# The norm of kk in a hybrid RWKV-7 and sliding-window attention block: products of 32 columns and a spread by 64-row products

## The chip, the cores and the metric

The kernel runs on one core of a Trainium2 chip. The metric is the device time of one execution in microseconds; lower is better. A core has a matrix engine (PE, whose weight loads are listed as PEld), a vector engine (DVE), a scalar engine (ACT), GpSimd (POOL) and a queue that issues transfers (SP). The engines run their own instruction lists and wait for each other on semaphores.

## The reference, cut to what matters

One decoder block over 1024 tokens and 2048 channels. Its projection feeds 16 RWKV-7 heads and 16 attention heads, all of 64 channels. Of the RWKV part the change touches this:

```python
kk = (k * k_k).reshape(B, T, H, N)                      # N = 64 channels of a head
kk = kk / jnp.maximum(jnp.linalg.norm(kk, axis=-1, keepdims=True), 1e-12)
...
xs = (r, decay, k, v, kk, kk * a)                       # each step of the recurrence
S = S * w_t + sa[..., None] * b_t + v_t[..., None] * k_t   # sa = -S kk_t, b_t = kk_t * a_t
```

The kernel leaves the factor kk * a without its norm and divides the other kk by the squared norm, which is the same product.

## The kernel before, in words

**Layout.** Channels lie on partitions and tokens on columns. The tokens are taken in two halves of 512 (`HALF`, four blocks `b` of 128). A pair of heads is one tile of 128 channels; there are 8 pairs, so 16 intervals `j` (0 to 15), of which the second half of the tokens has 8 to 15.

**The projection and its quarters.** All of the projection and output products go through `quarter` (L1113 is the helper `turn`, a transpose through PE; L1128 is the product of `quarter`). A tile of 128 output channels takes 16 chunks of 128 inputs, in four quarters of four chunks. Each chunk is three products of 128 x 512 (weights and x are split in a high and a low part). A quarter is so 12 products on L1128. The whole kernel is a loop over quarters `gq`, on every engine. An interval has 24 quarters; the number of the quarter within it is `at` in the code, and is called **step** here. Ahead of the 12 products of a step, PE does what `recurrence(j - 1, at)` and then `channels(j, at)` hand it: while interval j has its channels prepared, the recurrence and the attention of interval j - 1 are worked off in the same steps. For j = 0 there is no recurrence beside it, and after j = 15 the last recurrence runs with no channels.

**Pacing.** In step gq ACT makes the high part of the weights of quarter gq + 4 (`high`, L527), for which it waits until PE has finished quarter gq - 1 (its buffers are 5 deep), and DVE then makes the low part (`low`, L717), as its first instruction of the step. So DVE can't begin a step before PE has ended the one before.

**The norm of kk before.** ACT squares k * k_k at step 5 into `s1` (L590).
- Step 10, PE, L1167: for each of the four blocks, a product with the block of `s1` (128 x 128) as weights and the constant `head_of` (128 x 2) as what streams, into two columns of PSUM bank 2 each. A float32 product is two instructions, so these are 8. Result: tokens on partitions, 8 columns (4 blocks, 2 heads).
- Step 11, DVE, at its end: maximum with 1e-24 (L829), reciprocal (L830), copy with broadcast to 128 x 512 in `grow` (L831), then `inv_ready`.
- Step 12, PE, L1113 on the tile `work`: waits for `inv_ready`, four transposes of 128 x 128 from `grow` into bank 3.
- Step 13, DVE, L836: kk = k * k_k * bank 3, then `kk_read`. PE waits for `kk_read` at step 14 (L1280).

**What stands around it.** On PE: step 9 `turn_p(i, 0)`, eight transposes of the first half's attention probabilities (L1113 on `score`), which wait for `p_norm` that DVE gives at the end of `softmax_norm(i, 0)` (L915 to L918, signalled at L920) in step 8. Step 11: `values(i, 0)` (L1261), `turn_kk` (L1222) and level 0 of the inverse (L1271). Step 13: `turn_p(i, 1)`, which waits for the `p_norm` of `softmax_norm(i, 1)`, DVE's first work after `low` in step 12. On DVE: step 9 the output of an earlier interval (L1033, L1035) and scores; step 10 `softmax_top(i, 1)` (L903 to L909), then the eviction of the V tile (L735); step 11 `low`, `attended`, `shift` of v, and the norm.

**Tiles of PE.** Products with 64 columns or 64 rows of weights use a part of the array, and their neighbours another part: L1261 and L1349 have 128 rows x 64 columns (`128*64` in the rows), L1197 64 rows x 128 columns, L1222, L1271, L1280, L1338 and L1368 64 x 64.

**Constants.** `cst` is one tile of 1282 float32 columns, loaded at the start between the second and the third chunk of x. The first product that reads it is L1137 of the first quarter (sum of squares of x), which waits for its landing.

Of the kernel before, what the change touches and what calls it, by code (L numbers as in the profile page):

```python
# [10 lines left out]
ALU = mybir.AluOpType  # L11
# [3 lines left out]
P = 128  # L15
# [3 lines left out]
HD = 64  # L19
PAIRS = 8  # L20
# [46 lines left out]
CONSTS = {}  # L67
_at = 0
for _name, _w in (("ident", 128), ("same_head", 128), ("mean", 128), ("amask", 256), ("m16", 64),
                  ("m32", 64), ("dist", 256), ("dist0", 256), ("head_of", 2)):  # L70
    CONSTS[_name] = (_at, _at + _w)
    _at += _w
CONST_COLS = _at
# [2 lines left out]
def constants():  # L76
    r = np.arange(128)[:, None]
    c = np.arange(128)[None, :]
    t = {}
    t["ident"] = (r == c)  # L80
    t["same_head"] = (r // HD == c // HD)
    t["mean"] = np.full((128, 128), 1.0 / D)
    s, u = r % C, np.arange(C)[None, :]
    t["amask"] = np.concatenate([s <= u, s < u, s < u, s <= u], axis=1)
    for m in (16, 32):
        t[f"m{m}"] = (s // (2 * m) == u // (2 * m)) & (s % (2 * m) >= m) & (u % (2 * m) < m)
    key = np.arange(2 * BT)[None, :]
    d = BT + r - key
    t["dist"] = np.where((d >= 0) & (d < BT), d, 1e33)
    t["dist0"] = np.where((d >= 0) & (d < BT) & (key >= BT), d, 1e33)  # L90
    t["head_of"] = (r // HD == np.arange(2)[None, :])
    return np.concatenate([t[n].astype(np.float32) for n in CONSTS], axis=1)


# [13 lines left out]
def tile_of(i, t):  # L108
    return base(i) // 4 + tile_order(i).index(t)
# [41 lines left out]
def program(nc, io, scr):  # L151
    with ExitStack() as ctx:
        def sb(name, shape, dt=F32):
            return ctx.enter_context(nc.sbuf_tensor(name, shape, dt))
# [13 lines left out]
        own_stage = [sb(f"stage{i}", [P, HALF]) for i in range(3)]  # L168
        work = sb("work", [P, 8, HALF])
        k, a, s1, sw, grow, r, g, sig = (work[:, i] for i in range(8))  # L170
        raw = sb("raw", [P, HALF + 1])
        decay = sb("decay", [P, NCH, C + 1])
        lora = sb("lora", [P, HALF])
# [1 line left out]
        keep = sb("keep", [P, HALF], U8)  # L175
        carry = sb("carry", [P, 4 * PAIRS + 1])
        lora_up = [sb(f"lora_up{i}", [P, P]) for i in range(2)]
        inv2 = sb("inv2", [P, BH])
        pc = sb("pc", [P, 2, NCH])
        eps = sb("eps", [P, 2])  # L180
        sinks = sb("sinks", [P, HEADS])
# [137 lines left out]
        with nc.Block() as block:  # L319
# [387 lines left out]
            def _(dve):  # L707
                count = [0]

                def then(ins):  # L710
                    ins.then_inc(steps, 1)
                    count[0] += 1
                    dve.wait_ge(steps, count[0])
# [80 lines left out]
                def channels(j, at):  # L794
# [20 lines left out]
                    if at == 8:  # L815
# [2 lines left out]
                        then(nc.vector.tensor_tensor(kb[:, :, 0:4:3], a.rearrange(chunks, b=NB, c=2),  # L818
                                                     grow.rearrange(chunks, b=NB, c=2), ALU.mult))
                    if at == 10:  # L820
                        evicted(tile_of(j, V_T), h, 4 * n + 1)
                    if at == 11:
                        shift(v[:], p(n, "mu_v"))
                    if at == 12:
                        dve.wait_ge(s_full, 2 * j)
                        read_tile(tile_of(j, Q_T), q[:], HD ** -0.5)
                    if at == 11:
                        dve.wait_ge(norm_done, 2 * j + 1)
                        then(nc.vector.tensor_scalar(inv2[:], psum[:, 2, 0:BH], 1e-24, None, ALU.max))  # L829
                        then(nc.vector.reciprocal(inv2[:], inv2[:]))  # L830
                        then(nc.vector.tensor_copy(grow.rearrange("p (m d) -> p m d", d=HD),  # L831
                                                   inv2[:].unsqueeze(2).broadcast_to([P, BH, HD])))
                        dve.sem_inc(inv_ready, 1)
                    if at == 13:
                        dve.wait_ge(norm_done, 2 * j + 2)
                        then(nc.vector.scalar_tensor_tensor(k, k, p(n, "k_k"), psum[:, 3], ALU.mult, ALU.mult))  # L836
                        dve.sem_inc(kk_read, 1)
                        for c in range(2):
                            ins = nc.vector.tensor_tensor(
                                qr[:, :, 2 - c], k.rearrange(chunks, b=NB, c=2)[:, :, c],  # L840
                                decay[:, :, 0:C].rearrange("p (b c) t -> p b c t", c=2)[:, :, c], ALU.mult)
                        then(ins)
# [268 lines left out]
            def _(pe):  # L1111
# [28 lines left out]
                def channels(j, at):  # L1140
                    if at == 1:
                        h = j // PAIRS
                        pe.wait_ge(up_landed[j % 2], 16 * (j // 2 + 1))
                        pe.wait_ge(lora_ready, 2 * h + 2)
                        pe.wait_ge(rooted, h + 1)
                        pe.wait_ge(inv_ready, j)
                        pe.wait_ge(bonus_read, j)
                        if j == PAIRS:
                            pe.wait_ge(yt_read, PAIRS - 1)
                        for x in range(2):  # L1150
                            rows = slice(x * LORA, (x + 1) * LORA)
                            nc.tensor.matmul(psum[:, 2 + x], lora_up[j % 2][rows, :], lora[rows, :],
                                             start=True, stop=True).then_inc(lora_done, 1)
                    if at == 4 and j % PAIRS == 0:
                        h = j // PAIRS
                        pe.wait_ge(va_raw, h + 1)
                        pe.wait_ge(sigma_a, j + 1)
                        for b in range(NB):
                            mm = turn(psum[:, 3, b * P:(b + 1) * P], raw[:, 1 + b * P:1 + (b + 1) * P])
                        mm.then_inc(va_full, 1)  # L1160
                    if at == 10:
                        pe.wait_ge(squares, j + 1)
                        pe.wait_ge(sigma_w, j + 1)
                        if j >= 2:
                            pe.wait_ge(yt_read, j - 1)
                        for b in range(NB):
                            mm = nc.tensor.matmul(psum[:, 2, 2 * b:2 * b + 2], s1[:, b * P:(b + 1) * P],  # L1167
                                                  const("head_of"), start=True, stop=True)
                        mm.then_inc(norm_done, 1)
                    if at == 12:  # L1170
                        pe.wait_ge(inv_ready, j + 1)
                        pe.wait_ge(sigma_a, j + 1)
                        if j % PAIRS == 0:
                            pe.wait_ge(va_read, j // PAIRS + 1)
                        for b in range(NB):
                            mm = turn(psum[:, 3, b * P:(b + 1) * P], grow[:, b * P:(b + 1) * P])
                        mm.then_inc(norm_done, 1)
                    if at == 24:
                        pe.wait_ge(rkr_ready, j + 1)
                        pe.wait_ge(kk_read, j + 1)  # L1180
                        nc.tensor.matmul(psum[:, 3], const("same_head"), s1, start=True, stop=True  # L1181
                                         ).then_inc(bonus_done, 1)
# [296 lines left out]
```

## Time and profile before

| | us |
|---|---|
| median of 3 runs | 1952.3 |
| lowest, highest | 1951.01, 1953.26 |
| the profiled execution, its own time | 1952.34 |
| its span in the profile | 1950.6 |
| granted clock of PE, mean | 0.996 of full speed |

The span is that from the first to the last instruction; 1.7 us of the execution's time lie around it. In a row of the timeline the first number is the start in us from the span's start, the second the time from the first start to the last end of the instructions that the row merges, `x8` their count, and `[0.39 <-DVEq L920]` the idle time of that engine before them and what ended it. DVEq is DVE's sequencer: a semaphore raised at that line. PE's instructions overlap, since each is given its whole way through the array: what one costs is read from start to start, not from its duration.

### The profile page before, as it was taken

Reading aid. Unit: us, or ns where it says so; the run is one execution under the profiler, and the core shown is the slowest. Engines: PE = TensorE matmul, PEld = TensorE weight load, DVE = VectorE, ACT = ScalarE, POOL = GpSimd, SP = SyncE. Lnnn points to the kernel's source line nnn. Section 1 sums busy time; section 2 is a strip of 40 time slices with the busy share of each in tenths; the row PEclk is TensorE's granted clock in tenths of the full one; section 3 lists DMA queues with packets and bytes.
Section 4 is the critical chain, followed back from the end, with each engine's and each line's share of the span. In section 5 each row is a group of like instructions: output and inputs, shape, how many; then the busy total and the mean of one; then the engine's idle time right before and its main releaser. Section 6 shows DMA issues by size and latency. Waiting matters only on the chain.

```text
span 1950.6 us, 39494 instructions
## 1 busy us (share of the span) xinstructions
PE 1909.1 (98%) x16000; PEld 1542.0 (79%) x16000; DVE 1240.3 (64%) x2358; ACT 786.7 (40%) x1545; POOL 268.6 (14%) x585
## 2 busy tenths in 40 slices
PE   8999999999999999999999999999999999999996
PEld 5778878788788877788787877888787778888885
DVE  4667576767667677665767676676767764346433
ACT  6434434343434344444343434343434443243221
POOL 0002021120202020020211202020202021111110
PEclk9999999999999999999999999999999999999998
DMA  6533232323333234332323232232323543455533
GB/s 185 168 105 85 80 95 74 101 74 96 81 89 92 81 97 151 104 86 80 96 74 101 74 96 80 90 92 82 93 75 97 163 109 97 130 186 178 165 124 124
DMA packets 208453, 207.25 MB, mean 106 GB/s; under 512 B 114960, under 2 KB 117008, under 8 KB 208272
## 3 DMA queue, kind: packets, MB, share of 16 engines
q1 hardware_dynamic: 208272, 204.73, 35.2%
q8 instruction: 126, 2.06, 0.4%
q14 instruction: 55, 0.45, 0.1%
HBM read 181.08 MB, written 23.59 MB: 105 GB/s over the span
## 4 chain that ended last, share of the span: by engine, by line
PE 90%; DVE 6%; ACT 2%; issue 1%; DMA 1%; DVEq 0%; SPq 0%; ACTq 0%
PE psum L1128 70%; PE psum L1113 3%; PE psum L1280 2%; PE psum L1197 2%; PE psum L1236 2%; PE psum L1261 1%; PE psum L1271 1%; DVE w_lo L717 1%; DVE score L918 1%; PE psum L1385 1%; ACT w_hi L527 1%; PE psum L1349 1%; PE psum L1181 1%; PE psum L1356 1%; PE psum L1222 1%
## 5 line engine op out<-in xcount | busy, mean ns | idle before, releaser
L1128 PE MATMUL psum<-x_hi,w_hi 128*128 128x512 f32 x2144 | 885.3, 413 | 8.8 <-DVE x_lo L726 7.6
L1128 PE MATMUL psum<-x_hi,w_lo 128*128 128x512 f32 x2144 | 838.9, 391 | 0.0
L1128 PE MATMUL psum<-x_lo,w_hi 128*128 128x512 f32 x2144 | 836.0, 390 | 0.0
L717 DVE TENSOR_TENSOR w_lo<-w_raw,w_hi 128x512 fp32r<-128x512 f32 x536 | 373.8, 698 | 586.2 <-ACT w_hi L527 571.8
L527 ACT ACTIVATE w_hi<-w_raw 128x512 fp32r<-128x512 f32 x536 | 335.5, 629 | 845.8 <-PE psum L1128 838.3
L1128 PEld LDWEIGHTS psum<-x_hi,w_hi 128*128 128x128 f32 x2144 | 403.4, 188 | 108.9 <-DVE w_lo L717 17.4
L1128 PEld LDWEIGHTS psum<-x_hi,w_lo 128*128 128x128 f32 x2144 | 402.9, 188 | 88.8
L1128 PEld LDWEIGHTS psum<-x_lo,w_hi 128*128 128x128 f32 x2144 | 404.2, 189 | 80.5 <-issue 8.2
L474 POOL COPY xt<-sub_ident 64x256 f32<-64x256 f32 x16 | 9.2, 578 | 1013.7 <-DMA x<-scratch_L 1013.7
L482 POOL TENSOR_TENSOR xt<-xt,x 64x15 f32<-64x15 f32 (+7 forms) x240 | 97.5, 406 | 18.8
L480 POOL TENSOR_TENSOR x<-x,xt 64x15 f32<-64x15 f32 (+7 forms) x240 | 90.2, 376 | 18.8
L501 POOL TENSOR_TENSOR v<-v,kb 128x512 f32<-128x512 f32 x29 | 38.3, 1319 | 287.7 <-ACT kb L665 287.7
L527 ACT ACTIVATE states<-psum,pc 128x64 f32<-128x64 f32 x112 | 35.0, 313 | 103.4 <-PE psum L1385 103.2
L601 ACT ACTIVATE score<-score,top 128x256 f32<-128x256 f32 x128 | 63.3, 497 | 0.0
L527 ACT ACTIVATE late<-psum 64x256 f32<-64x256 f32 (+2 forms) x128 | 58.3, 482 | 1.1
L1385 PEld LDWEIGHTS psum<-states,score 128*128 128x128 f32 x256 | 48.4, 190 | 11.4 <-ACT states L527 0.9
L488 POOL MEMSET score<- 64x512 f32 x16 | 8.3, 518 | 305.4 <-PE psum L1113 305.3
L735 DVE TENSOR_TENSOR raw<-psum,rms 128x512 f32<-128x512 f32 x68 | 46.6, 686 | 2.4
L894 DVE SCALAR_TENSOR_TENSOR score<-cst,psum 128x256 f32<-128x256 f32 x128 | 45.1, 416 | 3.4 <-DVE ym L1035 3.4
L1385 PE MATMUL psum<-states,score 128*128 128x64 f32 x256 | 42.7, 247 | 0.0
L879 DVE TENSOR_TENSOR late<-psum,cst 128x512 f32<-128x512 f32 x64 | 41.1, 684 | 2.4
L1113 PE MATMUL psum<-cst,score 128*128 128x128 f32 x256 | 34.5, 278 | 7.6 <-DVEq L920 7.6
(238 smaller groups left out, 1911.2 us busy)
## 6 DMA issues: line engine op xcount, KB each, us to landing
w_raw<-in_w_in SPq DMA_DIRECT2D x408, 256.0 KB, 2.6
w_raw<-in_w_out SPq DMA_DIRECT2D x128, 256.0 KB, 2.6
stage<-in_x_t SPq DMA_DIRECT2D x20, 256.0 KB, 3.6
stage<-scratch_MIX SPq DMA_DIRECT2D x19, 256.0 KB, 4.1
scratch_L<-late SPq DMA_DIRECT2D x32, 128.0 KB, 2.6
x<-scratch_X SPq DMA_DIRECT2D x32, 128.0 KB, 3.2
x_t<-scratch_XT SPq DMA_DIRECT2D x32, 128.0 KB, 3.5
scratch_MIX<-sa SPq DMA_DIRECT2D x16, 256.0 KB, 3.1
```

Of the source, the lines that this page charges most:

```text
L480: then(nc.gpsimd.tensor_tensor(t, left, right, ALU.mult))
L482: then(nc.gpsimd.tensor_tensor(rows, rows, t, ALU.subtract))
L527: return nc.scalar.activation(dst, src, ACT.Copy, scale=scale)
L601: nc.scalar.activation(score[:, x], score[:, x], ACT.Exp, bias=top[:, 1, x:x + 1], accum_out=top[:, 2, x:x + 1])
L717: nc.vector.tensor_tensor(w_lo[gq % SPLIT][:], w_raw[gq % RAW][:], w_hi[gq % SPLIT][:].bitcast(F32), ALU.subtract).then_inc(w_ready, 1)
L735: then(nc.vector.tensor_tensor(dst, psum[:, s % 2], rms[s // H1][:], ALU.mult))
L879: ins = nc.vector.tensor_tensor(am[:, 2 * half:2 * half + 2, hh].rearrange("p b c x t -> p b (c x t)"), psum[:, bank].rearrange("p (b t) - ...
L894: ins = nc.vector.scalar_tensor_tensor(score[:, 2 * bb + hh], dist, -slope, psum[:, (6, 4)[rnd] + hh, bb * 2 * BT:(bb + 1) * 2 * BT], ALU. ...
L1113: return nc.tensor.transpose(dst, src, const("ident"))
L1128: mm = nc.tensor.matmul(psum[:, s % 2], wt[gq % SPLIT][:, cols], xx[:, c], start=(c == 0 and wt is w_hi and xx is x_hi), stop=(c == KC - 1 ...
L1197: mm = nc.tensor.matmul(dst.rearrange("p (x t) -> p x t", t=C), kb[rows, b, 2 * c:2 * c + 2].rearrange("p s t -> p (s t)"), qr[rows, b, c: ...
L1385: nc.tensor.matmul(psum[:, 6, m * HD:(m + 1) * HD], mt[:, m], states[:, m], start=False, stop=True, skip_group_check=True).then_inc(state_ ...
```

## The change

Constants: `head_of` gets 32 columns (the two columns of before, 16 times), and two new constants of 128 x 128, `even` and `odd`, pick a row. `cst` grows from 1282 to 1568 columns. The norm becomes:
- Step 9, PE, behind `turn_p(i, 0)`: four products with `head_of` (128 x 32) as weights and a block of `s1` (128 x 128) as what streams; block b goes to partitions 32 b to 32 b + 31 and columns 0 to 127 of bank 3. Heads are on partitions now, and tokens on columns.
- Step 10, DVE, ahead of the eviction of V: maximum and reciprocal of 128 x 128 into `inv` (the first 128 columns of `grow`), then `inv_ready`. The copy with broadcast is gone.
- Step 11, PE, behind level 0: waits for `inv_ready`; four products with 64 rows of `even` or `odd` as weights and 64 rows of `inv` as what streams, into banks 2 and 3, 256 columns each.
- Step 13, DVE: the same product as before, reading two banks.
- Steps 10 and 12 of PE are left without an insertion of `channels`.

```diff
--- before.py
+++ after.py
@@ -67,7 +67,8 @@
 CONSTS = {}
 _at = 0
 for _name, _w in (("ident", 128), ("same_head", 128), ("mean", 128), ("amask", 256), ("m16", 64),
-                  ("m32", 64), ("dist", 256), ("dist0", 256), ("head_of", 2)):
+                  ("m32", 64), ("dist", 256), ("dist0", 256),
+                  ("head_of", 32), ("even", 128), ("odd", 128)):
     CONSTS[_name] = (_at, _at + _w)
     _at += _w
 CONST_COLS = _at
@@ -88,7 +89,9 @@
     d = BT + r - key
     t["dist"] = np.where((d >= 0) & (d < BT), d, 1e33)
     t["dist0"] = np.where((d >= 0) & (d < BT) & (key >= BT), d, 1e33)
-    t["head_of"] = (r // HD == np.arange(2)[None, :])
+    t["head_of"] = (r // HD == np.arange(32)[None, :] % 2)
+    for name, first in (("even", 0), ("odd", 32)):
+        t[name] = (r % HD == first + c // HD)
     return np.concatenate([t[n].astype(np.float32) for n in CONSTS], axis=1)
 
 
@@ -168,6 +171,7 @@
         own_stage = [sb(f"stage{i}", [P, HALF]) for i in range(3)]
         work = sb("work", [P, 8, HALF])
         k, a, s1, sw, grow, r, g, sig = (work[:, i] for i in range(8))
+        inv = grow[:, 0:P]
         raw = sb("raw", [P, HALF + 1])
         decay = sb("decay", [P, NCH, C + 1])
         lora = sb("lora", [P, HALF])
@@ -175,7 +179,6 @@
         keep = sb("keep", [P, HALF], U8)
         carry = sb("carry", [P, 4 * PAIRS + 1])
         lora_up = [sb(f"lora_up{i}", [P, P]) for i in range(2)]
-        inv2 = sb("inv2", [P, BH])
         pc = sb("pc", [P, 2, NCH])
         eps = sb("eps", [P, 2])
         sinks = sb("sinks", [P, HEADS])
@@ -818,22 +821,21 @@
                         then(nc.vector.tensor_tensor(kb[:, :, 0:4:3], a.rearrange(chunks, b=NB, c=2),
                                                      grow.rearrange(chunks, b=NB, c=2), ALU.mult))
                     if at == 10:
+                        dve.wait_ge(norm_done, 2 * j + 1)
+                        then(nc.vector.tensor_scalar(inv, psum[:, 3, 0:P], 1e-24, None, ALU.max))
+                        then(nc.vector.reciprocal(inv, inv))
+                        dve.sem_inc(inv_ready, 1)
                         evicted(tile_of(j, V_T), h, 4 * n + 1)
                     if at == 11:
                         shift(v[:], p(n, "mu_v"))
                     if at == 12:
                         dve.wait_ge(s_full, 2 * j)
                         read_tile(tile_of(j, Q_T), q[:], HD ** -0.5)
-                    if at == 11:
-                        dve.wait_ge(norm_done, 2 * j + 1)
-                        then(nc.vector.tensor_scalar(inv2[:], psum[:, 2, 0:BH], 1e-24, None, ALU.max))
-                        then(nc.vector.reciprocal(inv2[:], inv2[:]))
-                        then(nc.vector.tensor_copy(grow.rearrange("p (m d) -> p m d", d=HD),
-                                                   inv2[:].unsqueeze(2).broadcast_to([P, BH, HD])))
-                        dve.sem_inc(inv_ready, 1)
                     if at == 13:
                         dve.wait_ge(norm_done, 2 * j + 2)
-                        then(nc.vector.scalar_tensor_tensor(k, k, p(n, "k_k"), psum[:, 3], ALU.mult, ALU.mult))
+                        halves = "p (x t) -> p x t"
+                        then(nc.vector.scalar_tensor_tensor(k.rearrange(halves, x=2), k.rearrange(halves, x=2),
+                                                            p(n, "k_k"), psum[:, 2:4, 0:2 * BT], ALU.mult, ALU.mult))
                         dve.sem_inc(kk_read, 1)
                         for c in range(2):
                             ins = nc.vector.tensor_tensor(
@@ -1158,22 +1160,27 @@
                         for b in range(NB):
                             mm = turn(psum[:, 3, b * P:(b + 1) * P], raw[:, 1 + b * P:1 + (b + 1) * P])
                         mm.then_inc(va_full, 1)
-                    if at == 10:
+                    if at == 9:
                         pe.wait_ge(squares, j + 1)
+                        pe.wait_ge(sigma_a, j + 1)
+                        pe.wait_ge(z_read, j)
+                        if j % PAIRS == 0:
+                            pe.wait_ge(va_read, j // PAIRS + 1)
+                        for b in range(NB):
+                            mm = nc.tensor.matmul(psum[32 * b:32 * b + 32, 3, 0:P], const("head_of"),
+                                                  s1[:, b * P:(b + 1) * P], start=True, stop=True,
+                                                  skip_group_check=True)
+                        mm.then_inc(norm_done, 1)
+                    if at == 11:
+                        pe.wait_ge(inv_ready, j + 1)
                         pe.wait_ge(sigma_w, j + 1)
                         if j >= 2:
                             pe.wait_ge(yt_read, j - 1)
-                        for b in range(NB):
-                            mm = nc.tensor.matmul(psum[:, 2, 2 * b:2 * b + 2], s1[:, b * P:(b + 1) * P],
-                                                  const("head_of"), start=True, stop=True)
-                        mm.then_inc(norm_done, 1)
-                    if at == 12:
-                        pe.wait_ge(inv_ready, j + 1)
-                        pe.wait_ge(sigma_a, j + 1)
-                        if j % PAIRS == 0:
-                            pe.wait_ge(va_read, j // PAIRS + 1)
-                        for b in range(NB):
-                            mm = turn(psum[:, 3, b * P:(b + 1) * P], grow[:, b * P:(b + 1) * P])
+                        for bb, name in enumerate(("even", "odd")):
+                            for x in range(2):
+                                rows = head_rows(x)
+                                mm = nc.tensor.matmul(psum[:, 2 + x, bb * P:(bb + 1) * P], const(name)[rows],
+                                                      inv[rows], start=True, stop=True)
                         mm.then_inc(norm_done, 1)
                     if at == 24:
                         pe.wait_ge(rkr_ready, j + 1)
```

## Rows read from the trace of the kernel before

**Rows 1.** The page: busy time of the engines.

```profile
PE 1909.1 (98%) x16000; PEld 1542.0 (79%) x16000; DVE 1240.3 (64%) x2358; ACT 786.7 (40%) x1545; POOL 268.6 (14%) x585
```

**Rows 2.** Waits of PE: us in total, times, longest.

```profile
PE psum L1113 <- DVEq L920: 7.6, 17, 1.5
...
PE psum L1113 <- DVEq L833: 1.5, 3, 1.1
```

**Rows 3.** Timeline of PE, interval 2, around step 10.

```profile
262.14 0.39 PE L1128 MATMUL psum<-x_hi,w_lo 128*128 128x512 f32 x1
262.37 0.95 PE L1167 MATMUL psum<-cst,work 128*128 128x2 f32 x8
...
263.49 0.39 PE L1128 MATMUL psum<-x_lo,w_hi 128*128 128x512 f32 x1
```

**Rows 4.** Timeline of PE, interval 2, steps 12 and 13.

```profile
271.32 0.39 PE L1128 MATMUL psum<-x_hi,w_lo 128*128 128x512 f32 x1
271.54 0.63 PE L1113 MATMUL psum<-cst,work 128*128 128x128 f32 x4
...
272.24 0.39 PE L1128 MATMUL psum<-x_lo,w_hi 128*128 128x512 f32 x1
...
274.76 1.07 PE L1113 MATMUL psum<-cst,score 128*128 128x128 f32 x8
```

**Rows 5.** Timeline of DVE, interval 2, steps 10 and 12.

```profile
266.95 0.69 DVE L735 TENSOR_TENSOR raw<-psum,rms 128x512 f32<-128x512 f32 x1
...
272.47 0.69 DVE L717 TENSOR_TENSOR w_lo<-w_raw,w_hi 128x512 fp32r<-128x512 f32 x1 [1.07 <-ACT w_hi L527]
...
273.48 1.14 DVE L918 TENSOR_SCALAR score<-score,part 128x256 f32<-128x256 f32 x4
```

**Rows 6.** Timeline, last recurrence, step 13: no channels beside it.

```profile
1603.78 1.14 DVE L918 TENSOR_SCALAR score<-score,part 128x256 f32<-128x256 f32 x4
...
1604.34 0.39 PE L1128 MATMUL psum<-x_hi,w_lo 128*128 128x512 f32 x1
...
1605.03 1.09 PE L1113 MATMUL psum<-cst,score 128*128 128x128 f32 x8 [0.31 <-DVEq L920]
```

**Rows 7.** Timeline of PE, last interval's products alone, 64 rows x 128 columns.

```profile
1559.40 0.39 PE L1128 MATMUL psum<-x_hi,w_lo 128*128 128x512 f32 x1
1559.72 2.06 PE L1197 MATMUL psum<-qr,kb 64*128 64x128 f32 x32
1561.71 0.50 PE L1128 MATMUL psum<-x_hi,w_hi 128*128 128x512 f32 x1
1562.04 0.39 PE L1128 MATMUL psum<-x_lo,w_hi 128*128 128x512 f32 x1
```

**Rows 8.** Timeline of PE, interval 2, step 11: tiles of 64 columns.

```profile
266.12 1.09 PE L1261 MATMUL psum<-pt,va 128*64 128x128 f32 x16
267.14 0.97 PE L1222 MATMUL psum<-cst,qr 64*64 64x64 f32 x26
...
268.69 0.50 PE L1128 MATMUL psum<-x_hi,w_hi 128*128 128x512 f32 x1
```

**Rows 9.** Groups of DVE by form: busy us, mean ns, idle before.

```profile
L925 DVE TENSOR_TENSOR sa<-sa,psum 128x256 f32<-128x256 f32 x32 | 13.2, 414 | 0.0
...
L772 DVE RECIPROCAL rms<-rms 128x512 f32<-128x512 f32 x1 | 3.4, 3353 | 0.0
L830 DVE RECIPROCAL inv<-inv 128x8 f32<-128x8 f32 x16 | 3.2, 203 | 0.5
```

**Rows 10.** Timeline of PE, interval 0, around step 12.

```profile
95.72 0.39 PE L1128 MATMUL psum<-x_hi,w_lo 128*128 128x512 f32 x1
...
97.97 0.39 PE L1128 MATMUL psum<-x_lo,w_hi 128*128 128x512 f32 x1
```

**Rows 11.** Timeline of PE at the start: the constants.

```profile
10.15 2.07 PE L1137 MATMUL psum<-work,cst 128*128 128x512 f32 x2 [0.95 <-DMA cst<-in_consts]
```

**Rows 12.** Stretches: busy us and count by engine, PEclk, DMA share, GB/s.

```profile
5.00:10.00 5.00, 1.62 (x3) 0.84 (x3) 2.09 (x3) 3.33 (x6) 0.00 (x0) 1.00 0.95 315
```

## The prediction

> **What bounds the kernel now.** I read the page first: PE is busy for 98% of the span, with DVE at 64% [rows 1]. So every insertion on PE counts from start to start, and a saving on DVE counts only where PE waits for DVE. The waits of PE say where that is [rows 2]: nearly all of its waiting beyond the start is for `p_norm` (L920), 17 times, ahead of the transposes of the probabilities; the `inv_ready` of this change (L833) was waited for 3 times, 1.5 us in all. The timelines of PE and DVE around steps 9 to 13 then give the price of each insertion and the slack of each wait. The products on L1128 follow each other every 0.23 us (eleven of those steps lie between 272.24 and 274.76 [rows 4]; I use 0.227, which is their pace where nothing is inserted). What an insertion costs is the distance from the last L1128 start before it to the second one after it, less two of these.
>
> The sum is made against the profiled execution, 1952.34 us (span 1950.6), which is 0.04 over the median of 1952.3. About 0.2%, 3.9 us, is what a measurement of this kernel can tell from no change.
>
> **What is removed.** Step 10: the eight instructions of L1167 cost 263.49 - 262.14 - 0.45 = 0.90 us [rows 3]. Their 2 columns stream in no time; they are paced by loading 128 x 128 weights eight times. Step 12: the four transposes cost 272.24 - 271.32 - 0.45 = 0.47 us [rows 4].
>
> **But the 0.47 us are covered already.** In step 12 DVE first makes the low weights, which it can't before PE has ended step 11, and then `softmax_norm`; its last multiplication ends at 273.48 + 1.14 = 274.62, and PE starts `turn_p` at 274.76, 0.14 later [rows 5, 4]. In the last recurrence, which has no transposes in step 12, PE waits for the same signal: the multiplication ends at 1604.92, PE starts at 1605.03, 0.11 later, and 0.69 after its last product instead of 0.23 [rows 6]. So 0.11 is the latency of the signal, and the slack in interval 2 is 0.03 us. Without the transposes PE arrives 0.47 earlier and waits 0.44: the saving of step 12 is 0.03 us, and a new wait on L920 in step 13 is what is late next. Everything between the end of step 11 and `turn_p` of step 13 hangs on DVE, so what is moved from step 12 to step 11 turns from free into paid.
>
> **Step 9, the four products with 32 columns.** The trace has no product of 128 x 32. It has two neighbours. Sixteen instructions of 128 x 64 that stream 128 columns take 1.02 us up to the next kind [rows 8], 0.064 each, against 0.11 for transposes of the full array that stream as many: two run at once. Taking out 0.09 for the change of tile shape (0.32 from the last L1128 to the first L1197 instead of 0.23 [rows 7]) and some 0.05 for the first start, a round of two takes 0.11. If four tiles of 32 columns run at once, the eight instructions are two rounds: 0.09 into the tiles + 0.05 + 0.22 + 0.09 out + 0.11 for the first L1128 after tiles (0.33 instead of 0.23 [rows 7]) = 0.57 us. If only two do, four rounds: 0.79. If none, eight rounds: 1.22. I take 0.57, because in both tiled forms that are nearest all the tiles that the form allows run side by side. The Trainium skill, "TensorEngine Tiling (Array Packing)", section Tiling Modes, lists 128 x 32 as four independent tiles; by that it would be 0.57 as well, and no row here shows it.
>
> **Step 11, the spread.** The row for 64 x 128 with 128 streamed columns: 32 instructions of L1197, 16 rounds of two, from 1559.40 to 1562.04, less 0.45, are 2.19 us [rows 7]. Less 0.34 for shape changes and first starts, a round is 0.115. Four rounds behind level 0, whose own way in and out is paid already: 0.09 + 0.05 + 0.46 = 0.60 us. Bounds: 0.46 if the change from 64 x 64 to 64 x 128 costs nothing, 1.06 if the pairs don't overlap.
>
> **Does the spread wait?** DVE now has 128 columns where it had 8, and a reciprocal is slow: 203 ns for 8 columns, 3353 for 512 [rows 9], 6.24 ns a column, so 0.95 us for 128. The maximum from PSUM is about 0.28 (414 ns for 256 [rows 9], with a third of that fixed). It starts where the eviction of V did, 266.95 [rows 5]; 0.28 + 0.03 + 0.95 + 0.11 of signal give 268.32. PE would be ready for the spread where L1128 starts now, 268.69 [rows 8], less 0.90, plus 0.57: 268.36. So it just fits; in intervals where DVE is later by a few tenths, as in the two that waited for L833 in step 12, the wait comes back here instead of being saved. I count zero for both together. The eviction of V and the rest of DVE's step 11 come 1.3 us later, less the three instructions that go from its end, among them the old reciprocal and a copy of 512 columns; DVE had 1.07 idle before step 12 [rows 5], so what is left of it hides there. The Trainium skill, "VectorE: DVE Perf Modes", in the part on what is physically there per lane, has the reciprocal repeat its divide 8 times; at 8 cycles of the 0.96 GHz that the Trainium skill gives for the engine, a column would take 8.3 ns and the 128 columns 1.2 us. The rows disagree: 6.24.
>
> **The sum.** Intervals 1 to 15: +0.57 + 0.60 - 0.90 - 0.03 = +0.24 us each, **+3.6**. Interval 0 has no recurrence and no `p_norm`: its step 12 costs 97.97 - 95.72 - 0.45 = 1.80 with its wait [rows 10], step 10 another 0.90. New: 0.58 + 0.80 for two insertions alone, and an allowance of 0.2 for a wait, since DVE starts its step 10 only after PE's step 9. **-1.1**. Constants: 286 columns more are 0.146 MB; the first product that reads them waits for them for 0.95 [rows 11], while the engines move 315 GB/s [rows 12]: **+0.45** (between 0 and 1.0; PE is the pace from there on). SP issues the same transfers in the same order. Together +2.95, some +3: **1955.3 us**, 0.15% slower, within what can't be told.
>
> **The rivals.**
> - *The products are not four at once* (slower). Place: step 9. Only two at once costs 0.22 more, in 16 intervals +3.5 us: 1958.8; one at a time +10.4: 1965.7. It decides from two at once. For it: 128 x 64 and 64 x 64 tiles never have more than two streams over the same rows, and four streams over all 128 rows read twice as much as any row here. Against it: no tiled form in the trace falls behind its number of tiles. Chance 0.2.
> - *The spread waits for DVE* (slower). The fit above is 0.04 us wide, in the 13 intervals that have an earlier output and the probabilities in DVE's way. With the maximum at its bound of 0.41 it would be missed by 0.09, +1.2 us in all; I price the rival at DVE being 0.25 later than I have it, 13 x 0.25, less the 0.04: +2.7 us, 1958.0. It decides from 0.1 us on. Against it: the durations of the rows. Chance 0.1. By the rule of the Trainium skill on the reciprocal, above, it would be this case.
> - *The saving of step 12 is real* (faster). If the wait for `p_norm` does not take its place, 0.44 in 15 intervals come back, 6.6 us: 1948.7. For it: PE shows no waits there now. Against it: rows 6, the same step without the transposes, and the 0.03 of slack. It could also come true if DVE got earlier in step 12, which nothing moves. Chance 0.08.
> - That the change doesn't do what it says is the first rival; the order of work moves in any case.
>
> **How the numbers follow.** Forecast 0.62, with its own range of 1953 to 1957.5, since each 0.1 us in one insertion is 1.6 us; a quarter of it lies above 1956.2. Slower: 0.3 from the two slower rivals nearly whole, 0.15 from the forecast: 0.44. Faster 0.08. The same 0.48. The range goes from 1951.5, where constants and switches cost nothing, to 1960, over both slower rivals at their prices; left out are the full third rival and products one at a time.
>
> **What would show it.** Right: L1128 to L1128 over step 9 longer by about 0.57, over step 11 by 0.60; idle time of PE on L920 up from 17 times to some 31, about 0.44 us longer each from start to start in step 13; the reciprocal at 0.95. Wrong: step 13's transposes start 0.23 after the last product (third rival), or the eight instructions of step 9 come in more than two clusters of starts (first), or PE waits for the new `inv_ready` in most intervals (second).

## The result, and the profile after

The changed kernel takes 1956.87 us (median of 10 runs, 1955.02 to 1957.80) against 1951.55 for the kernel before (10 runs, 1950.10 to 1953.26): ratio 1.0025, 95% interval 1.0015 to 1.0034. That is 5.3 us slower, more than the 3.9 that count as no change. The profiled execution took 1956.89, its span 1955.1. The loading at the start of a span differs by about a microsecond between executions, of the same kernel too (experiment 1), so the traces are compared below from the first L1128 of quarter 12 on: to that of quarter 420 it is 1541.3 us before and 1547.2 after.

The page says nothing moved: PE is as busy as before.

```profile
PE 1908.2 (98%) x16064; PEld 1532.0 (78%) x16064; DVE 1246.3 (64%) x2342; ACT 786.2 (40%) x1545; POOL 264.1 (14%) x585
```

The waits of PE say more (columns as in [rows 2]): 32 waits for `p_norm`, 13.8 us, where there were 17 with 7.6.

```profile
PE psum L1115 <- DVEq L922: 13.8, 32, 1.5
...
PE psum L1182 <- DVEq L827: 0.7, 2, 0.3
```

The lines have moved by two or three: L1115 is `turn`, L1130 the product of a quarter, L1170 the norm products, L1182 the spread, L922 `p_norm`, L827 `inv_ready`; on ACT L530 is `high`, on DVE L720 `low`. The timeline of PE in interval 2, steps 8 and 9:

```profile
255.74 0.39 PE L1130 MATMUL psum<-x_hi,w_lo 128*128 128x512 f32 x1
256.51 1.09 PE L1115 MATMUL psum<-cst,score 128*128 128x128 f32 x8 [0.38 <-DVEq L922]
257.53 0.43 PE L1170 MATMUL psum<-work,cst 128*32 128x128 f32 x8
257.89 0.50 PE L1130 MATMUL psum<-x_hi,w_hi 128*128 128x512 f32 x1
258.23 0.40 PE L1130 MATMUL psum<-x_lo,w_hi 128*128 128x512 f32 x1
```

The eight instructions of 32 columns are over in 0.36 us, from 257.53 to 257.89, the way out included. Step 11, its end:

```profile
265.73 0.46 PE L1278 MATMUL psum<-x,late 64*64 64x64 f32 x14
266.19 0.72 PE L1182 MATMUL psum<-work,cst 64*128 64x128 f32 x8
266.84 0.50 PE L1130 MATMUL psum<-x_hi,w_hi 128*128 128x512 f32 x1
267.17 0.40 PE L1130 MATMUL psum<-x_lo,w_hi 128*128 128x512 f32 x1
```

And step 13, which had its transposes 0.23 us behind the last product [rows 4] and now has them 0.77 behind:

```profile
272.18 0.39 PE L1130 MATMUL psum<-x_hi,w_lo 128*128 128x512 f32 x1
272.95 1.09 PE L1115 MATMUL psum<-cst,score 128*128 128x128 f32 x8 [0.38 <-DVEq L922]
273.80 0.48 PE L1130 MATMUL psum<-x_hi,w_hi 128*128 128x512 f32 x1
```

DVE in the same interval, steps 10 and 12:

```profile
264.80 0.29 DVE L825 TENSOR_SCALAR work<-psum 128x128 f32<-128x128 f32 x1
265.12 0.95 DVE L826 RECIPROCAL work<-work 128x128 f32<-128x128 f32 x1
...
270.69 0.69 DVE L720 TENSOR_TENSOR w_lo<-w_raw,w_hi 128x512 fp32r<-128x512 f32 x1 [0.91 <-ACT w_hi L530]
...
271.70 1.14 DVE L920 TENSOR_SCALAR score<-score,part 128x256 f32<-128x256 f32 x4
```

Counted over all intervals in the way of the prediction (from the last product of the step before to the second product of this one, less 0.454 us), PE's insertions are, in us:

| step | before | after | difference | forecast |
|---|---|---|---|---|
| 9, intervals 1 to 15 | 22.25 | 30.91 | +8.7 | +8.6 |
| 10 | 13.62 | 0 | -13.6 | -13.5 |
| 11 | 41.55 | 52.73 | +11.2 | +9.0 |
| 12 | 7.86 | 0 | -7.9 | together |
| 13 | 13.61 | 22.30 | +8.7 | -0.5 |
| 14 | 35.74 | 35.34 | -0.4 | 0 |
| interval 0, all | 2.70 | 1.51 | -1.2 | -1.1 |

That is +5.5; the rest of the 5.9 between the two stretches is what small differences elsewhere, of both signs, add up to (the insertions of the other steps and the pace between the products), and no experiment looked into them. What step 12 lost came back in step 13, and more.

### The profile page after: what moved, and what is told of

The parts are those of the page before. It is cut to its first block, busy times and chain, and to the rows that moved or that the text cites. A ratio compares the mean times of both kernels' runs of the same rounds, so it can differ in the third digit from the quotient of the medians.

```text
span 1955.1 us, 39608 instructions
## 1 busy us (share of the span) xinstructions
PE 1908.2 (98%) x16064; PEld 1532.0 (78%) x16064; DVE 1246.3 (64%) x2342; ACT 786.2 (40%) x1545; POOL 264.1 (14%) x585
## 4 chain that ended last, share of the span: by engine, by line
PE 88%; DVE 7%; ACT 2%; issue 1%; DMA 1%; DVEq 0%; SPq 0%; ACTq 0%
PE psum L1130 69%; PE psum L1115 3%; PE psum L1287 2%; DVE score L920 2%; DVE w_lo L720 2%; PE psum L1204 2%; PE psum L1243 2%; PE psum L1268 2%; PE psum L1278 1%; ACT w_hi L530 1%; PE psum L1392 1%; PE psum L1356 1%; PE psum L1188 1%; PE psum L1363 1%; PE psum L1229 1%
## 5 line engine op out<-in xcount | busy, mean ns | idle before, releaser
L1130 PE MATMUL psum<-x_hi,w_hi 128*128 128x512 f32 x2144 | 882.1, 411 | 9.3 <-DVE x_lo L729 7.5
L1130 PE MATMUL psum<-x_hi,w_lo 128*128 128x512 f32 x2144 | 838.8, 391 | 0.0
L1130 PE MATMUL psum<-x_lo,w_hi 128*128 128x512 f32 x2144 | 837.0, 390 | 0.0
L720 DVE TENSOR_TENSOR w_lo<-w_raw,w_hi 128x512 fp32r<-128x512 f32 x536 | 373.7, 698 | 585.1 <-ACT w_hi L530 569.1
L530 ACT ACTIVATE w_hi<-w_raw 128x512 fp32r<-128x512 f32 x536 | 335.5, 629 | 842.0 <-PE psum L1130 834.8
L1130 PEld LDWEIGHTS psum<-x_hi,w_hi 128*128 128x128 f32 x2144 | 403.0, 188 | 115.4 <-DVE w_lo L720 17.3
L1130 PEld LDWEIGHTS psum<-x_hi,w_lo 128*128 128x128 f32 x2144 | 402.7, 188 | 88.4
L1130 PEld LDWEIGHTS psum<-x_lo,w_hi 128*128 128x128 f32 x2144 | 403.9, 188 | 81.7 <-issue 7.7
L530 ACT ACTIVATE states<-psum,pc 128x64 f32<-128x64 f32 x112 | 35.2, 314 | 104.3 <-PE psum L1392 104.1
L530 ACT ACTIVATE late<-psum 64x256 f32<-64x256 f32 (+2 forms) x128 | 58.3, 482 | 1.1
L1115 PEld LDWEIGHTS psum<-cst,score 128*128 128x128 f32 x256 | 27.5, 141 | 27.3 <-DVEq L922 27.3
L1115 PE MATMUL psum<-cst,score 128*128 128x128 f32 x256 | 35.0, 280 | 13.8 <-DVEq L922 13.8
L530 ACT ACTIVATE pt<-psum 128x512 f32<-128x512 f32 x64 | 34.8, 596 | 26.7 <-PE psum L1115 26.7
```

The costliest lines, as they stand in the source:

```text
L530: return nc.scalar.activation(dst, src, ACT.Copy, scale=scale)
L720: nc.vector.tensor_tensor(w_lo[gq % SPLIT][:], w_raw[gq % RAW][:], w_hi[gq % SPLIT][:].bitcast(F32), ALU.subtract).then_inc(w_ready, 1)
L1115: return nc.tensor.transpose(dst, src, const("ident"))
L1130: mm = nc.tensor.matmul(psum[:, s % 2], wt[gq % SPLIT][:, cols], xx[:, c], start=(c == 0 and wt is w_hi and xx is x_hi), stop=(c == KC - 1 ...
```

## The experiments

In the order of what they ask. Each is a change of the kernel before or of the changed kernel; the medians have 5 to 11 runs behind them and stand beside runs of the kernel before on the same chip (1951.4 to 1951.7).

**1. The changed kernel again.**

> The changed kernel once more, on the chip of these runs, as their measure: 5 us over the kernel before. From the fifth quarter on (59 us) to the last recurrence (1601 us in the kernel before) it takes some 6 us more; the first 37 us differ between executions by 1 to 2 us in either direction.

Measured: 1956.85, ratio 1.0026 (1.0017 to 1.0036). From quarter 12 to 420 it takes 1547.1, as the first time. The span starts differ: the first L1130 of quarter 12 is at 58.2 here and 59.2 there.

**2. The kernel before without the transposes of step 12.**

```diff
                     if at == 12:
                         pe.wait_ge(inv_ready, j + 1)
...
-                        for b in range(NB):
-                            mm = turn(psum[:, 3, b * P:(b + 1) * P], grow[:, b * P:(b + 1) * P])
-                        mm.then_inc(norm_done, 1)
```

On DVE the product of step 13 reads `grow` in place of bank 3, and its waits are adapted.

> The kernel before without the four transposes of step 12, its wait for inv_ready kept; the product of step 13 reads the untransposed factor, so the output is another. Theory (step 12 is covered by DVE's way to p_norm): the transposes of step 13 start 0.11 us after the last multiplication on DVE in every interval, a wait of some 0.45 us appears there, and the time falls by 1 to 2 us only (0.45 in interval 0, some 0.4 in each of intervals 6 and 14, 0.02 in the others). Rival (an insertion costs its length wherever it stands): 16 x 0.46, -7.3 us.

Measured: 1949.57, ratio 0.9992 (0.9983 to 1.0001). Step 12 falls from 7.86 to 1.40 (what is left are waits for `inv_ready`), and step 13 rises from 13.61 to 19.39. Of 6.5 us, 5.8 are back one step later, as waits for `p_norm` (here L919), now 31 of them in the view of PE's waits:

```profile
PE psum L1112 <- DVEq L919: 10.9, 31, 1.5
```

The four transposes were all but free where they stood: the transposes of step 13, which followed the last product after 0.23 us in the kernel before, follow it after 0.58 to 0.70 in 14 of the 15 intervals. Measured from quarter 12 to 420 it is 1.7 us less than before. The rival of -7.3 us is out.

**3. The changed kernel with the spread in step 12.**

```diff
-                    if at == 11:
+                    if at == 12:
                         pe.wait_ge(inv_ready, j + 1)
```

> The changed kernel with the spread in step 12 instead of step 11. Theory: step 11 loses 0.71 us, step 12 gains 0.85 (a tiled group by itself), of which 0.55 lies in the wait for p_norm that step 13 has now; net -0.41 in 15 intervals, -6.1 us on the changed kernel, which is 1 us under the kernel before (-0.5 to -1.5). Rival (the spread costs its length anywhere): +2 us on the changed kernel, 7 over the kernel before.

Measured: 1949.04, ratio 0.9992 (0.9983 to 1.0000): 7.8 under the changed kernel. Step 11 is back at 41.55, step 12 costs 12.72 (0.85 each), and step 13 falls from 22.30 to 13.31. The waits for `p_norm` in step 13 are gone, with the same work on every engine. In interval 2 the transposes of step 13 carry no wait:

```profile
268.38 0.72 PE L1182 MATMUL psum<-work,cst 64*128 64x128 f32 x8
...
271.89 1.03 PE L1115 MATMUL psum<-cst,score 128*128 128x128 f32 x8
```

The theory had -6.1: it took 0.71 for step 11, where the mean is 0.745, and 0.55 for the wait that is filled, where step 13 falls by 0.60 in the mean, since of transposes that had to wait the second also starts later after the first (0.165 us in the changed kernel, 0.108 here, in interval 2). The slot, not the form of the products, is what the change lost by.

**4. The changed kernel without the reciprocal.**

```diff
-                        then(nc.vector.tensor_scalar(inv, psum[:, 3, 0:P], 1e-24, None, ALU.max))
-                        then(nc.vector.reciprocal(inv, inv))
+                        then(nc.vector.tensor_scalar(inv, psum[:, 3, 0:P], 1e-24, 4e-10, ALU.max, ALU.mult))
```

> The changed kernel without the reciprocal on DVE (the maximum and a constant factor in one instruction take its place, so the output is another). Theory: the spread in step 11 starts without a wait, 0.15 instead of 0.22 us after the last product of level 0, and what it still costs is the shape change and the array's own time: -0.07 us in 11 intervals and -0.4 in the two where it waits longest, -1.6 us on the changed kernel; the step still costs 0.64 to 0.65. Rival (the spread's cost above 0.60 is waiting for DVE altogether): step 11 falls to 0.60.

Measured: 1955.98, ratio 1.0026 (1.0016 to 1.0036). Step 11 falls from 52.73 to 51.29 and is 3.42 us in each of the 15 intervals, 0.65 over the kernel before's 2.77. So of the spread's 0.745 on average, 0.65 are the array's and 0.095 are waits for the reciprocal. Of the forecast -1.6 us, 1.4 are seen in step 11 and 0.8 from quarter 12 to 420. The rival, 0.60, is out: the array's own time was mis-sized.

**5. The norm products in step 8, the spread left in step 11.**

```diff
-                    if at == 9:
+                    if at == 8:
                         pe.wait_ge(squares, j + 1)
```

> The changed kernel with the norm products in step 8 instead of 9, the spread left in step 11. Theory: step 8's 0.56 us are covered by the wait for p_norm in step 9, so PE would be 0.55 us earlier at the spread; but inv_ready hangs on DVE, whose steps 8 to 10 are one unbroken chain behind p_norm, and PE already waits 0.07 for it. The wait in step 11 grows to some 0.6 us and the saving is gone: 0 to -1 us on the changed kernel. Rival (the cover alone decides): -0.54 in 15 intervals, -8 us.

Measured: 1956.93, ratio 1.0025 (1.0016 to 1.0035), as the changed kernel. Steps 8 and 9 together fall from 30.91 to 22.35, by 8.6, and step 11 rises from 52.73 to 59.64, by 6.9; the 1.6 us between the two don't show in the medians, and from quarter 12 to 420 only 0.5 of them are seen. The wait has moved to `inv_ready`, in the timeline of interval 2 and in the sum of PE's waits:

```profile
266.20 0.71 PE L1182 MATMUL psum<-work,cst 64*128 64x128 f32 x8 [0.51 <-DVEq L827]
```

```profile
PE psum L1182 <- DVEq L827: 7.1, 13, 0.9
```

So between the step-9 transposes and the spread PE is held by DVE's chain from `p_norm` over the older output, the scores and the top to the reciprocal, in which DVE has no pause of over 0.22 us in interval 2.

**6. Both moved: norm products in step 8, spread in step 12.** The edits of 3 and 5 together.

> The changed kernel with the four norm products in step 8 instead of 9 and the spread in step 12 instead of 11: both insertions stand in a step behind which PE waits for p_norm. Theory: step 9 loses 0.55 us, step 8 gains 0.58, of which 0.55 are covered by the wait for p_norm in step 9; with the -0.41 of the spread -0.93 in 15 intervals, -14 us on the changed kernel, some 8.6 under the kernel before. Rival (length counts anywhere): step 8 for step 9 changes nothing, the spread +0.14: 7 us over the kernel before.

Measured: 1943.62, ratio 0.9959 (0.9947 to 0.9972), 7.8 under the kernel before and 13.3 under the changed one. Alone, the two moves gave 0 and -7.8: the first pays only once the spread no longer waits behind DVE's chain. The norm products in step 8 cost 8.35 us in 15 intervals and save 8.7 of waiting in step 9 (13.53 now, 22.25 in the kernel before). What is left of waits on `p_norm`, in the view of PE's waits:

```profile
PE psum L1115 <- DVEq L922: 2.5, 5, 1.5
```

**7. A semaphore increment at the end of DVE's step 11.**

```diff
                     if at == 11:
                         shift(v[:], p(n, "mu_v"))
+                        dve.sem_inc(v_ready, 1)
```

> The changed kernel with one semaphore increment on DVE behind the shift of v, at the end of step 11, that nobody waits for. In the kernel before the increment of inv_ready stood there, and the low weights of step 12 started 33 ns after ACT's high part; in the changed kernel it is 108 ns, with a separate semaphore instruction in between. Theory (two waits in a row on DVE need an instruction of their own, and the increment takes up the first): back to 33 ns, -0.075 us in 15 intervals, -1.1 us on the changed kernel. Rival (the 108 ns come from the shape of the preceding work, as in step 8): 0.

Measured: 1955.64, ratio 1.0021 (1.0013 to 1.0030), 1.2 under the changed kernel. Step 13 falls from 22.30 to 21.15. In the timelines of DVE and ACT, step 12 of interval 2, DVE starts at 270.75 where ACT's high part began at 270.09 and lasts 0.63:

```profile
270.75 0.69 DVE L721 TENSOR_TENSOR w_lo<-w_raw,w_hi 128x512 fp32r<-128x512 f32 x1 [0.86 <-ACT w_hi L531]
```

```profile
270.09 0.63 ACT L531 ACTIVATE w_hi<-w_raw 128x512 fp32r<-128x512 f32 x1 [1.53 <-PE psum L1132]
```

In the changed kernel the same two stand at 269.95 and 270.69, 0.08 further apart. What takes them apart is a separate semaphore instruction of DVE. The subtraction of `low` has two waits: one for ACT's high part (the line above it, L719 in the changed kernel), one for `steps`, the completion of DVE's own last instruction. Where an increment stands in between, it takes up the wait for `steps`. Where none does, a semaphore instruction takes the wait for ACT, and the subtraction follows it. The changed kernel has 125 of these instructions, one more in each of the 15 intervals than the kernel before (110, on L716); with the increment they are 110 again:

```profile
L719 DVEq EVENT_SEMAPHORE  x125: 21/21/21, 5.9 to 1785.8; - x125
```

```profile
L720 DVEq EVENT_SEMAPHORE  x110: 21/21/21, 5.9 to 1787.4; - x110
```

So the removal of DVE's three instructions and of their `inv_ready` from the end of step 11 made `p_norm` of step 13 late by 0.075 us in 15 intervals, 1.1 us. The difference of the medians alone would not carry this, and from quarter 12 to 420 the profiled execution is even 0.7 us longer than that of the changed kernel (1547.8; one wait of step 19 is longer by 1.9); the distances in every interval do carry it (31 to 33 against 107 to 108 ns).

**8. The same increment in the kernel before, at the end of step 7.**

> The kernel before with one semaphore increment on DVE at the end of step 7, which nobody waits for, so that the low weights of step 8 start 32 ns after ACT's high part instead of 108, as they do in step 12. Theory: p_norm of step 9 comes 0.075 us earlier in 15 intervals, -1.1 us, and the distance from the last product of step 8 to the transposes falls from 775 to 700 ns. Rival: the 108 ns stay, 0.

Measured: 1950.27, ratio 0.9993 (0.9984 to 1.0002). The mechanism is there: DVE has 95 of the semaphore instructions instead of 110, the transposes of step 9 follow the last product after 698 ns instead of 775, and step 9 falls from 22.25 to 21.09. The medians can't tell the gain from none, and from quarter 12 to 420 only 0.5 us of the 1.1 are seen.

**9. The kernel before with its own norm products in step 8 and bank 3.**

```diff
-                    if at == 10:
+                    if at == 8:
...
-                            mm = nc.tensor.matmul(psum[:, 2, 2 * b:2 * b + 2], s1[:, b * P:(b + 1) * P],
+                            mm = nc.tensor.matmul(psum[:, 3, 2 * b:2 * b + 2], s1[:, b * P:(b + 1) * P],
```

DVE's maximum in step 11 reads bank 3 as well.

> The kernel before, with its eight weight-bound instructions of the norm in step 8 instead of 10 and in bank 3 instead of 2 (bank 2 is still being read there). Theory: step 10 loses 0.91 us, step 8 gains 0.91 of which 0.55 are covered by the wait for p_norm in step 9: -0.55 in 15 intervals, -8.2 us on the kernel before. Rival: moving them changes nothing, 0.

Measured: 1948.18, ratio 0.9985 (0.9976 to 0.9994), 3.3 under the kernel before, not 8.2. Step 9 falls by 9.0 as forecast, but step 12 rises from 7.86 to 15.59, on `inv_ready` (L833), which comes at the end of DVE's step 11 (PE's waits):

```profile
PE psum L1113 <- DVEq L833: 7.2, 14, 1.1
```

My expectation had left this out; experiment 5 then showed the same on the changed kernel.

**10. The same, with the three DVE instructions of the reciprocal in step 10.**

```diff
                     if at == 10:
+                        dve.wait_ge(norm_done, 2 * j + 1)
+                        then(nc.vector.tensor_scalar(inv2[:], psum[:, 3, 0:BH], 1e-24, None, ALU.max))
+                        then(nc.vector.reciprocal(inv2[:], inv2[:]))
+                        then(nc.vector.tensor_copy(grow.rearrange("p (m d) -> p m d", d=HD), ...))
+                        dve.sem_inc(inv_ready, 1)
                         evicted(tile_of(j, V_T), h, 4 * n + 1)
```

The same instructions are taken out of `if at == 11`.

> The kernel before with its norm products in step 8 and bank 3, as in the run with the old norm in step 8, and with the three small DVE instructions of the reciprocal moved from the end of step 11 to step 10, ahead of the eviction of V. Theory: what ate the gain there was inv_ready, which came at the end of DVE's step 11 while PE stood at step 12 some 0.5 us earlier (7.2 us of waits on it); two steps earlier on DVE that wait is gone and the transposes of step 12 are covered by the way to p_norm: -0.55 in 15 intervals, -8 us on the kernel before, and 1.8 to 2 for interval 0's wait less. Rival (the waits on inv_ready only show what p_norm of step 13 would have taken): as that run, -3.3 us.

Measured: 1942.15, ratio 0.9949 (0.9936 to 0.9961), 9.5 under the kernel before: the quickest median of all, with the old form of the norm. Its interval overlaps with that of experiment 6; from quarter 12 to 420 it takes 1531.8, where experiment 6 takes 1533.7. So once both sit in free slots, the new form shows no advantage over the old one. Step 12 is 6.71 now, transposes without waits, and interval 0's is 0.44 instead of 1.79. The timeline of PE in interval 2, steps 8, 9, 12 and 13, shows no wait any more:

```profile
250.53 0.95 PE L1167 MATMUL psum<-cst,work 128*128 128x2 f32 x8
254.21 1.04 PE L1112 MATMUL psum<-cst,score 128*128 128x128 f32 x8
...
266.06 0.60 PE L1112 MATMUL psum<-cst,work 128*128 128x128 f32 x4
269.33 1.09 PE L1112 MATMUL psum<-cst,score 128*128 128x128 f32 x8
```

A small one is still there, below what the view marks: the transposes of step 13 start 0.28 to 0.31 us after the last product in every interval, 0.23 in the kernel before. By moving the three instructions this run, too, took the increment of `inv_ready` away from the end of step 11, and DVE starts step 12 107 to 109 ns behind ACT, as in experiment 7. No run has this placement with an increment left there.

**11. The constants alone.** The kernel before with `cst` of 1568 columns.

> The kernel before with the 286 further columns of constants and nothing else. Theory: the first product that reads them waits longer by what 0.146 MB take at 315 GB/s, +0.45 us on the kernel before. Rival: the landing at the start varies by more than that, as the changed kernel's shorter wait (0.7 instead of 0.95 us) suggests, and the constants cost nothing: 0 within 0.3 us.

Measured: 1952.44, ratio 1.0004 (0.9996 to 1.0013). The wait of the first product that reads them is 1.22 us here, 0.73 in the changed kernel, 0.95 in the kernel before [rows 11]; the timelines of PE at the start, first of this run and then of the changed kernel:

```profile
10.21 2.08 PE L1139 MATMUL psum<-work,cst 128*128 128x512 f32 x2 [1.22 <-DMA cst<-in_consts]
```

```profile
9.87 2.08 PE L1139 MATMUL psum<-work,cst 128*128 128x512 f32 x2 [0.73 <-DMA cst<-in_consts]
```

Neither 0 nor 1 us can be excluded; this term stays open.

## Why the prediction was right, and where it was off

The forecast was 1955.3, +3 us, within a range that holds the measured 1956.87; of its three chances, 0.48 for no change and 0.44 for slower, it was the second that came. The direction and the covered slot were right; the size that was forecast is about half of the measured one, because two terms below were both too small. Point by point:

- **Step 9, the products of 32 columns: right.** The first rival is out: the eight instructions start in two clusters of four (257.534 to 257.553 and 257.667 to 257.687 us in interval 2), and alone in interval 0 they cost 0.557 us for the 0.57 to 0.58 forecast. The 15 intervals have 8.66 us for the 8.6 of the sum. This agrees with what the Trainium skill, "TensorEngine Tiling (Array Packing)", section Tiling Modes, lists for 128 x 32: four tiles.
- **The covered slot of step 12: right.** Experiment 2 shows it on the kernel before, experiment 3 on the changed one. The third rival (the saving is real) is out. In step 13 the transposes come 0.54 us later after the last product than before, where the prediction had 0.44.
- **Its size was off.** The sum had -0.03 us for steps 12 and 13 together, measured is +0.055 (0.8 us over 15 intervals). The step that failed is "Everything between the end of step 11 and `turn_p` of step 13 hangs on DVE", which is right, taken with DVE's time of before: DVE's first instruction of step 12 starts 0.075 us later behind ACT than it did, since nothing at the end of step 11 takes up the pending wait (experiment 7).
- **The spread was mis-sized**: "Four rounds behind level 0", at 0.60 us. The array takes 0.65 (experiment 4). I had put 0.05 for the first start of a tiled group, from 64 columns; with 64 rows x 128 columns of weights the second pair starts 0.21 after the first instead of 0.16 for 128 x 64, and the rounds are 0.112. Sixteen rounds of L1197 hid this in their mean.
- **The spread waits a little**, where the prediction had "it just fits". It missed by 0.06 in most intervals and by 0.41 in two, 1.4 us in all (52.73 less 51.29). The two terms on DVE were as forecast, 0.29 and 0.95 us. Counted from the transposes of step 9, `inv_ready` came 0.03 later than the sum had it and PE 0.08 sooner. The second rival was so partly true, at half its price. The prediction's estimate of 1.2 us for the reciprocal, worked out from the repeat count of 8 that the Trainium skill, "VectorE: DVE Perf Modes", gives, does not hold here: it is 0.95 us for 128 columns, as the rows of before gave.
- **Interval 0: right**, -1.19 for -1.1. **Constants: open**; no run shows the +0.45.
- **One reading was too strong.** "Nearly all" of PE's waiting beyond the start was not for `p_norm`: that was 7.6 us of some 19. The others are single waits (3.2 us on L1007 in two, 2.9 on L860 in three), none of them for anything that the change moves but the 1.5 on `inv_ready`, so the sum does not suffer.

With 0.745 for 0.60 in step 11 (+2.2), +0.055 for -0.03 in steps 12 and 13 (+1.3) and the constants left out (-0.45), the sum of 2.95 becomes 6.0; the stretches differ by 5.9, the medians by 5.3.

Why the change, which takes more out of PE than it puts in, gains nothing is settled by experiments 2, 3 and 6. It takes 0.91 us out of a slot that is paid and 0.52 out of one that was covered, and puts 0.58 and 0.745 into paid slots. The two slots that PE has free in an interval are ahead of the two `turn_p`, steps 8 and 12, 0.55 to 0.6 us each.

## What to carry to other kernels

Work inserted on the bounding engine costs its length only where that engine does not wait shortly behind it: find the waits first, and put movable work into the steps ahead of them. A move pays only if what it feeds is early too; the chain on the other engine that makes its input has to be moved with it (experiment 5 gave 0, experiment 9 gave 3.3 of the 8.2 us forecast, 6 and 10 nearly the whole). The price of a form read from a long group hides its first round and its change of shape, which are some 0.2 of the 0.65 us of the spread's four rounds.

## What was not expected of the hardware

- A second wait ahead of an instruction on DVE costs 0.075 us here: 108 ns from the end of ACT's instruction to the start of DVE's with two waits in front, 32 with one. An increment that nobody waits for, put where it takes up the first wait, removes it (experiments 7 and 8).
- Loads of 32 columns of weights take 106 to 109 ns against 188 for 128 columns, and the products of four such tiles start 6 to 7 ns apart. The loads of L1170 in interval 2 (min, median and max in ns):

```profile
L1170 PEld LDWEIGHTS psum<-work,cst x8: 106/108/109, 257.5 to 257.6; 128*32 128x32 f32 x8
```

- The start of a program is its least certain part: quarter 12 of the changed kernel began at 58.2 us in one profiled execution and at 59.2 in another, twice what the constants were forecast to cost.
